# A hybrid decoder layer on one core: modulation weights loaded ahead of x, index scores a unit later with a block in each tile, counts turned later, and the last head's half added ahead of the products

## What is computed

```python
mod = jax.nn.silu(c) @ w_ada + b_ada
shift, scale, gate = jnp.split(mod, 3, axis=-1)
h = rmsnorm(x, norm_in) * (1.0 + scale[:, None, :]) + shift[:, None, :]
(cb, cc, cu, cz, aq, ak, av, az, iq, ik, iw) = jnp.split(h @ w_in, cuts, axis=-1)
y_conv = group_rmsnorm(cb * conv(cc * cu), gn_conv, 8) * jax.nn.silu(cz)
# q, k, q_idx, k_idx are rotated by position (the first 16 of 64 dimensions)
score = sum over 8 index heads of w_idx * relu(q_idx . k_idx)       # causal
_, sel = lax.top_k(score, 256)                 # for every query, in blocks of 128
y_attn = softmax attention of 8 heads over the chosen keys
y_attn = group_rmsnorm(y_attn, gn_attn, 8) * jax.nn.silu(az)
return rmsnorm(x + gate[:, None, :] * (concatenate([y_conv, y_attn]) @ w_out), norm_f)
```

## Time and profile before

| | us |
|---|---|
| median of 3 runs | 781.19 (779.42 to 783.22) |
| the profiled execution | 780.36 |
| its span, first to last instruction | 778.6 |
| PE busy | 674.9 (87%) |
| DVE / ACT / POOL busy | 471.5 / 360.5 / 230.1 |

### The profile page before, as it was taken

The page is one execution under the profiler, slowest core; times in us unless marked ns, Lnnn a source line. Parts: engine busy times, 40 slices in busy tenths (PEclk is TensorE's granted clock), DMA queues, the critical chain, the costliest instruction groups (busy, mean ns, idle before and its releaser), DMA issues.

```text
span 778.6 us, 8765 instructions
## 1 busy us (share of the span) xinstructions
PE 674.9 (87%) x3170; PEld 550.7 (71%) x3170; DVE 471.5 (61%) x734; ACT 360.5 (46%) x542; POOL 230.1 (30%) x111
## 2 busy tenths in 40 slices
PE   0459993989999999639999999999889989879995
PEld 0447993768888888537887877787777777658884
DVE  3677822778889999955802210003788989566734
ACT  3554432755643223413244443344787877773211
POOL 0032322035324225531765656460011310030000
PEclk9967996999999999969999999999999999989998
DMA  8901189024325211100113411124964440211431
GB/s 341 367 28 54 48 218 154 1 81 136 103 88 165 80 55 54 33 22 28 54 63 128 162 55 32 50 64 104 297 154 113 111 106 4 57 55 68 174 109 54
DMA packets 22517, 79.14 MB, mean 102 GB/s; under 512 B 3722, under 2 KB 4042, under 8 KB 21452
## 3 DMA queue, kind: packets, MB, share of 16 engines
q1 hardware_dynamic: 22476, 78.60, 33.3%
HBM read 61.77 MB, written 13.41 MB: 97 GB/s over the span
## 4 chain that ended last, share of the span: by engine, by line
PE 55%; DVE 28%; DMA 5%; issue 5%; ACT 4%; SPq 2%; DVEq 0%; POOL 0%; ACTq 0%
PE ps L615 10%; PE ps L616 10%; PE ps L617 10%; DVE above L1232 7%; PE ps L790 4%; PE ps L792 4%; PE ps L791 4%; PE ps L728 3%; DMA xin<-in_x 2%; PE ps L673 2%; PE ps L674 2%; PE ps L654 2%; DMA iqs<-hlL 2%; PE ps L655 2%; DVE acc L1130 2%
## 5 line engine op out<-in xcount | busy, mean ns | idle before, releaser
L615 PE MATMUL ps<-hH,wH 128*128 128x512 f32 (+1 forms) x592 | 234.2, 396 | 8.4 <-DVE hL L430 4.4
L616 PE MATMUL ps<-hL,wH 128*128 128x512 f32 (+1 forms) x592 | 229.6, 388 | 0.0
L617 PE MATMUL ps<-hH,wL 128*128 128x512 f32 (+1 forms) x592 | 229.5, 388 | 0.0
L1451 POOL TENSOR_TENSOR wL<-raw,wH 128x1024 fp32r<-128x1024 f32 x37 | 93.7, 2534 | 219.1 <-ACT wH L852 219.0
L615 PEld LDWEIGHTS ps<-hH,wH 128*128 128x128 f32 x592 | 112.6, 190 | 33.9 <-issue 11.7
L617 PEld LDWEIGHTS ps<-hH,wL 128*128 128x128 f32 x592 | 112.7, 190 | 21.7
L616 PEld LDWEIGHTS ps<-hL,wH 128*128 128x128 f32 x592 | 113.1, 191 | 19.8 <-issue 1.0
L1317 DVE CUSTOM_DVE_ANT_0 ps<-ps,bias 128x128 f32<-128x128 f32 (+3 forms) x64 | 48.7, 761 | 57.1 <-PE ps L655 55.2
L1325 DVE TENSOR_TENSOR phL<-ps,phH 128x512 fp32r<-128x512 f32 (+1 forms) x96 | 52.7, 555 | 23.9 <-ACT phH L1007 19.1
L987 ACT ACTIVATE relu<-ps,wabs 128x384 f32<-128x384 f32 (+5 forms) x48 | 40.0, 849 | 46.8 <-PE ps L674 27.1
L1232 DVE TENSOR_SCALAR_CACHE_REDUCE above<-score,srch 128x384 bf16<-128x384 f32 (+5 forms) x60 | 56.8, 946 | 2.1
(11 more groups left out here) (193 smaller groups left out, 1073.5 us busy)
## 6 DMA issues: line engine op xcount, KB each, us to landing
raw<-in_w_units SPq DMA_DIRECT2D x36, 512.0 KB, 3.4
wa<-in_w_ada SPq DMA_DIRECT2D x8, 1024.0 KB, 13.3
ks<-qk_halves SPq DMA_DIRECT2D x32, 256.0 KB, 5.5
xin<-in_x SPq DMA_DIRECT2D x8, 512.0 KB, 12.5
gw<-in_w_ada SPq DMA_DIRECT2D x8, 512.0 KB, 4.9
qs<-qk_halves SPq DMA_DIRECT2D x16, 256.0 KB, 3.9
wo<-in_w_out SPq DMA_DIRECT2D x8, 512.0 KB, 9.2
xe<-in_x SPq DMA_DIRECT2D x8, 512.0 KB, 4.1
```

Source lines behind the costliest of these rows:

```text
L615: pe.matmul(out, wH[:, n % 2, kt, :], hH[:, kt, cols], start=(kt == 0), stop=False)
L616: pe.matmul(out, wH[:, n % 2, kt, :], hL[:, kt, cols], start=False, stop=False)
L617: mm = pe.matmul(out, wL[:, n % 2, kt, :], hH[:, kt, cols], start=False, stop=(kt == KT - 1))
L1451: g.tensor_tensor(wL[:, n % 2, :, :], raw[:, n % NRAW, :, :], wH[:, n % 2, :, :].bitcast(F32), ALU.subtract).then_inc(s_wL, 1)
```

## The change

The front: w_ada is loaded whole before x, and x is squared, rooted and normalized in groups of 4, 2, 1 and 1 tiles. PE adds up the modulation first and turns x afterwards; no copy of the turned x is made. ACT makes five tiles of h straight out of PSUM with scale and shift, DVE the tiles 1, 4 and 6 (`H_DVE`), ACT makes all hH, DVE all hL and POOL none. Before unit 0 PE does all 64 transposes, in three PSUM pairs, each of which must have been read before it is used again.

The scores: one block in each of aq1, aq2, aq3, ak1, ak2, ak3; the rotation of ak0 stands before block 2 and no longer behind block 3; the turned rows of iq0 are read back at iq3 instead of aq0. The counts: "most" behind cz1 and cc2, the gate's loads at cz2, cc3, cu3, cb3, its turning behind cz3, its row's way out at az1. The end: `head_out(15)` stands ahead of the scalings, block 3's first part is split into high and low within the last head, early steps are spread otherwise, and block 7 is finished in two halves.

```diff
-        ("aq", 0): [("idx", 2), ("idx", 3)],
-        ("ak", 0): [("idx", 4)],
...
+        ("ak", 0): [("idx", 2)],
+        ("aq", 1): [("idx", 3)],
...
-        ("cb", 0): [("most", 0)],
-        ("cz", 0): [("most", 1)],
-        ("cb", 3): [("gate", 0)],
+        ("cz", 1): [("most", 0)],
+        ("cc", 2): [("most", 1)],
+        ("cz", 3): [("gate", 0)],
...
+SCORES_IN = {UNIT[u]: (i, 1, 4 if i == 2 else 0)
+             for i, u in enumerate((("aq", 1), ("aq", 2), ("aq", 3), ("ak", 1), ("ak", 2), ("ak", 3)), 2)}
+GATE_IN = {UNIT[u]: kt for kt, u in zip(range(0, KT, 2), (("cz", 2), ("cc", 3), ("cu", 3), ("cb", 3)))}
+H_DVE = (1, 4, 6)
+X_GROUPS = ((0, 4), (4, 6), (6, 7), (7, 8))
...
-EARLY_PARTS = {3: 2, 4: 2, 5: 2, 6: 2, 7: 2, 8: 2, 10: 2, 11: 2}
+EARLY_PARTS = {4: 2, 5: 2, 6: 2, 7: 3, 8: 3, 10: 2, 11: 2}
...
-                if UNITS[n] == ("aq", 0):
+                if UNITS[n] == ("iq", 3):
                     sp.wait_ge(s_spill[0], spilled(0))
...
+            for t in range(NB):
+                pe.wait_ge(s_xn, t + 1)
+                for kt in range(3):
+                    mm = turn_x(kt, t)
+                    if t == NB - 1:
+                        mm.then_inc(s_xtp, 1)
+            for kt in range(3, KT):
+                wait_h(pe, kt - 3)
+                for t in range(NB):
+                    mm = turn_x(kt, t)
+                mm.then_inc(s_xtp, 1)
...
+            for kt in range(KT):
+                if kt not in H_DVE:
+                    act.wait_ge(s_xtp, kt + 1)
+                    A(xT[:, kt, :], two(2 + 2 * (kt % 3)), ACT.Identity, bias=shift[:, kt:kt + 1],
+                      scale=amp[:, kt:kt + 1]).then_inc(s_hA, 1)
+                wait_h(act, kt)
+                A(hH[:, kt, :], xT[:, kt, :], ACT.Copy).then_inc(s_hH, 1)
             split_high(1)
...
+            make_h(H_DVE[0])
+            for kt in range(KT):
+                if kt + 2 in H_DVE:
+                    make_h(kt + 2)
+                dve.wait_ge(s_hH, kt + 1)
+                v.tensor_tensor(hL[:, kt, :], xT[:, kt, :], hH[:, kt, :].bitcast(F32), ALU.subtract).then_inc(s_hL, 1)
...
             rotate(TURN_AT[("aq", 0)])
+            rotate(TURN_AT[("ak", 0)])
...
-                if i == 3:
-                    rotate(TURN_AT[("ak", 0)])
...
+            b = NB - 1
+            dve.wait_ge(s_xe[1], 16 * (b // 2 + 1))
+            dve.wait_ge(s_fsq, b)
+            for half in range(2):
+                cols = slice(HALF * half, HALF * half + HALF)
+                if half:
+                    dve.wait_ge(s_op, NB)
+                else:
+                    dve.wait_ge(s_oph, 1)
+                v.tensor_tensor(te[:, 1, cols], ps[:, out_pair(b) + half, :], gate[:, cols], ALU.mult).then_inc(s_teh, 1)
```

More of the change, by code:

```diff
@@ L232, in build @@
         finr = small[:, 48:56]
+        finh = small[:, 56:58]
+        squares = at("squares", [P, 4, D], F32, 32)
         xin = at("xin", [P, NB, D], F32, 113)
@@ L424, in wait_low, with wait_h @@
                 waits.wait_ge(s_splP, m + 1 - NT)
-        def low_h(engine, waits, kt, done):
-            waits.wait_ge(s_h, kt + 1)
-            waits.wait_ge(s_hH, kt + 1)
-            engine.tensor_tensor(hL[:, kt, :], xT[:, kt, :], hH[:, kt, :].bitcast(F32), ALU.subtract).then_inc(done, 1)
+        def wait_h(waits, kt):
+            if kt in H_DVE:
+                waits.wait_ge(s_hD, H_DVE.index(kt) + 1)
+            else:
+                waits.wait_ge(s_hA, kt + 1 - sum(x < kt for x in H_DVE))
         block = ctx.enter_context(nc.Block())
@@ L450, in _ @@
             for kt in range(KT):
-                if kt == 3:
-                    for t in range(NB):
-                        sp.dma_start(xin[:, t, :], a["x"][0, P * t:P * t + P, :]).then_inc(s_x[t], 16)
                 if kt >= 4:
@@ L563, in _ @@
             sp.dma_start(gate[:], dgate.rearrange("(o n) -> o n", o=1).broadcast_to([P, D])).then_inc(s_gate, 16)
-            for b in range(NB):
+            for b in range(NB - 1):
                 sp.wait_ge(s_fin, b + 1)
@@ L569, in _ @@
                     sp.dma_start(xe[:, b % 2, :], a["x"][0, P * (b + 2):P * (b + 3), :]).then_inc(s_xe[b % 2], 16)
-            for i in range(2):
-                sp.wait_ge(s_out[i], 16 * (NB // 2))
+            for half in range(2):
+                sp.wait_ge(s_finh[half], 1)
+                cols = slice(HALF * half, HALF * half + HALF)
+                sp.dma_start(a["out"][0, P * (NB - 1):P * NB, cols], oe[:, 1, cols]).then_inc(s_out[1], 16)
+            sp.wait_ge(s_out[0], 16 * (NB // 2))
+            sp.wait_ge(s_out[1], 16 * (NB // 2 + 1))
         @block.tensor
@@ L593, in _, with turn_x @@
             mm.then_inc(s_modp, 1)
+            def turn_x(kt, t):
+                return pe.transpose(two(2 + 2 * (kt % 3))[:, P * t:P * t + P], xin[:, t, P * kt:P * kt + P], identF[:])
+            for t in range(NB):
[6 more added lines that the diff above has]
+                wait_h(pe, kt - 3)
+                for t in range(NB):
+                    mm = turn_x(kt, t)
+                mm.then_inc(s_xtp, 1)
             def unit(n):
@@ L610, in unit @@
                             pe.wait_ge(s_hH, kt + 1)
-                            if kt in HL_POOL:
-                                pe.wait_ge(s_hLp, HL_POOL.index(kt) + 1)
-                            else:
-                                pe.wait_ge(s_hL, kt + 1 - sum(k < kt for k in HL_POOL))
+                            pe.wait_ge(s_hL, kt + 1)
                         pe.matmul(out, wH[:, n % 2, kt, :], hH[:, kt, cols], start=(kt == 0), stop=False)
@@ L1081, in _ @@
                     high(2, 0)
+                    high(3, 0)
                 if k == LAST // 2 + 10:
@@ L1087, in _ @@
             pair_root(NT - 1, 0)
-            high(3, 0)
             for ct in LATE_OUT:
@@ L1094, in _, with last_block @@
             pair_root(NT - 1, 1)
+            def last_block():
+                for half in range(2):
+                    act.wait_ge(s_resh, half + 1)
+                    cols = slice(HALF * half, HALF * half + HALF)
+                    A(xe[:, 1, cols], te[:, 1, cols], ACT.Square, accum_out=finh[:, half:half + 1]).then_inc(s_fsq, 1)
+                act.wait_ge(s_fv, NB)
+                A(finr[:, NB - 1:NB], fin[:, NB - 1:NB], ACT.Sqrt, scale=1.0 / D, bias=vec[:, V_EPS:V_EPS + 1]).then_inc(s_fs, 1)
+                act.wait_ge(s_fr, 1)
+                act.wait_ge(s_rnh, 2)
+                A(oe[:, 1, HALF:D], oe[:, 1, HALF:D], ACT.Copy, scale=finr[:, NB - 1:NB]).then_inc(s_finh[1], 1)
             for b in range(NB):
```

131 lines of the change are left out of this document (70 added, 61 removed).

## The result

| | before | after |
|---|---|---|
| median of the runs, us | 780.64 (779.42 to 783.22) | 736.28 (735.85 to 738.53) |
| profiled execution, its span | 778.6 | 734.0 |
| mean granted clock | 0.96 | 0.99 |

The ratio is 0.9424, its 95% interval [0.9395, 0.9453]: 5.8% faster. The forecast was 731.0 with a range of 722 to 742, so the sign and the range hold. The sum of the gains was 50.3 us and the spans differ by 44.6. Four cuts through the two traces say where the missing 5.7 went. They are the start of unit 1, PE's first transpose of a block of attention weights (`prob`), the start of the last matmuls of the output, and the end.

A forecast was written before the change was run, and what follows sets the result against it. PE, busy 87% of the span, was taken as the bound, standing still in four places. Gains of 7.8, 12.9, 2.3, 19.4, 5.0, 1.0 and 1.9 sum to 50.3 us: span 778.6 to 728.3, median 731 us, range 722 to 742.

The forecast's parts named there:

- The counts: PE's 17.6 us wait behind cb0 for DVE's count vanishes, plus 1.8 of clock: gain 19.4 us, bounds 14 to 19.4.
- The rival of a longer search: DVE's search stretches beside POOL's work until the count is late again and bounds PE: 737 us, chance 0.10.
- The slices: PE's 12.0 us wait in ak0 for slices of iq nearly vanishes, with its clock loss: gain 12.9 us, bounds 8 to 13.8.
- The start: Before unit 0, ACT's chain of h ends sooner, last hL at 57.5 us against 65.7: gain 7.8, bounds 5 to 10.
- The scores: PE's 3.8 us of relu waits shrink to some 1.5 at block 2: gain 2.3 us, bounds 0 to 3.8.
- The tail: At the attention's end, the squares' wait goes, some 2.2 us for DVE's sum remain: gain 5.0 us, bounds 3 to 7.
- The early steps: Early output steps no longer stand where PE waits 1.8 us for ACT: gain 1.0 us, bounds 0 to 2.5.
- The last block: Block 7's closing full-width steps are done in halves, ending sooner: gain 1.9 us, bounds 1.2 to 2.5.
- The queue: The iq slices are bound by the DMA queue and land only 3 us earlier: 736 to 738 us, chance 0.10.
- The start gains nothing: ACT's chain runs 0.6 us a step slower than added up, hL ends at 65: 738 to 739 us, chance 0.10.
- Slower by SP's wait: SP's wait for the masks at cz2 delays cb3's weights, about 791 us if masks come at 475; chance 0.02.

The follow-up runs named there:

- e2: Changed kernel with scores and the read-back of iq0's rows put back where they stood before, counts left as changed: 748.45 us.
- e1: Changed kernel with only the new start kept, everything else as before the change: 768.46 us, ratio 0.9858 to the kernel before.
- e8: Changed kernel with block 2's scores from step 8 of aq1 instead of 4, and POOL's low part of aq0 held until six scores are done: 742.43 us.
- e10: e7 plus block 2's scores from step 8 of aq1 instead of 4, and aq0's low part made by DVE instead of POOL: 725.86 us.
- e6: Changed kernel with DVE's gate of the last half pair ahead of the four scalings and its sum ahead of w_out's low part: 730.73 us.
- e7: e6 plus POOL's two last low parts of w_out given to DVE, so POOL has no work in the tail: 729.47 us.
- e4: Changed kernel with the end of the attention and the early steps put back as before the change: 734.82 us.
- e3: Changed kernel with the turned counts and the gate's sums put back where they stood before: 772.12 us, ratio 0.9882 to the kernel before.
- e5: Changed kernel with block 7 of the output finished whole instead of in two halves: 737.83 us.

## Why the prediction was right, and where it was not

The total came within 5.3 us, but in part because errors cancel: the start, the slices and the last block gave some 3 us more than forecast, the scores, the counts and the end of the attention with the early steps some 9 us less.

**The counts, right.** Forecast 19.4, measured alone 18.3 to 18.7, with its mechanism: PE is at the count at 358.8, as computed, and the masks are done at 405.2 (forecast 403). The slack was 12.5 us instead of 17, because the count was there at 346.3, not at 341.4: the search started 3.1 us later than computed, and DVE's last row for the count took 2.25 us where it had 0.17 before. The rival of a longer search came only to that extent: 113.7 us from the search's first row to the count's, against 114.0.

**The slices, right, but by the luck of less than 1 us.** No wait for them is left, so the term stands at its upper bound of 13.8, or near it: e2, which takes back slices and scores together, loses 12.2. The forecast kept 1.1 us of the wait "by the old landing". The landing moved some 11.9 us (134.3 to 122.4) instead of the 7.8 plus 0.2 that I gave it: the start gained more (below), and the queue the rest, with a spread of some 0.6 us between executions. The credit for the read-back at iq3 was right to be small: no effect beyond that spread can be seen.

**The start, right, undersized.** 9.9 for 7.8. The last hL was computed for 57.5 and came at 56.05. The step that was off is the roots: I had ACT's squares follow the landings, x7's root near 40.2, but it ended at 38.98, since a square and its read-out took some 1.15 one behind the other, less than the 1.28 that I set. The chain of h took 13.9 us, as forecast, by two errors that cancel: the passes that read PSUM with scale and bias from a tile took 1.19 to 1.21 and not 1.03, and the high parts in a row 1.00 and not 1.06. Of the missing 2.1 us, this is 1.45. Another 0.4 was lost in writing the forecast down: its own 65.7 less 57.5 is 8.2, not 7.8. The last 0.2 is unit 0, 6.4 us from the last hL to unit 1 in place of 6.6; PE's clock is 1.00 from 30 us on (0.52 from 45 to 62 us before), but before it waited for hL anyway and had caught up as well. And e1 shows the part alone at 12.2, 2.4 of it by a search that ran shorter.

**The scores, wrong in size: 2.3 forecast, nothing gained.** The step that failed is "PE stops for some 1.5 us". It stopped for 3.07 and then ran at a granted clock of 0.83 over ten us in the profiled execution. I had put the rotation's last addition in at 3.29 but its neighbours at their own times; DVE's first score behind it, 0.41 by itself, took 2.49 beside POOL's low part. e8 and e10 show that: take POOL's instruction away and the row is 0.41. The trace of before had the same pair right behind the row, and the forecast did not use it:

```profile
159.62 2.65 DVE L1206 TENSOR_SCALAR score<-relu,wsgn 128x640 f32<-128x640 f32 x1
158.58 3.35 POOL L417 TENSOR_TENSOR hlL<-T,hlH 128x1024 fp32r<-128x1024 f32 x1
```

**The tail, wrong in size: 5.0 forecast, next to nothing gained.** The four scalings and the sum were right. The step that failed is "the gate (0.7), a low part of w_out (1.25 [...], longer while POOL works)". The words had the cause and the number left it out: they took 2.90 and 3.37, 4.3 us more than the 1.95 summed. The trace of before had both instructions, in this same tail and beside work of POOL:

```profile
693.95 2.06 DVE L1377 TENSOR_TENSOR hL<-wo,woB 128x1024 fp32r<-128x1024 f32 x1
695.93 2.85 DVE L1355 SCALAR_TENSOR_TENSOR ya<-ya,vec,azs 128x512 f32<-128x512 f32 x1
```

With these two prices, 4.91 us for the 1.95, the sum lands 3.0 us later and the wait for it is 5.2 instead of 2.2, more than the 4.0 of the squares that it replaces; it measured 4.86. (The forecast's terms add up to 695.3 where it wrote "near 696"; from 695.3 the wait would be 4.4.) That the cause is POOL is shown (e6: 0.75 for the same gate; e7: four low parts at 1.2). The rule cited with the search, that a DVE instruction with two SBUF inputs and a GpSimd one that reads SBUF exclude each other for the whole instruction (the Trainium skill, SBUF — State Buffer, Who interferes with whom), holds for the gate and the low part, and belonged in this term. The first score is no exception to it: the same section counts `tensor_scalar` among the operations that can take the shared ports with one SBUF input, and the 2.49 us beside POOL against 0.41 alone agree.

**The early steps** were not measured apart; with the tail they brought 0.8 of 6.0, and e4, which takes both back, is as fast.

**The last block, right.** 2.2 for 1.9.

**The rivals.** "The queue" came within 0.3 to 0.7 us of deciding. "The start gains nothing" is disproved by e1. "Slower by SP's wait" needed masks 62 us late; they were 2 us late. That the parts do not add up was nowhere in the forecast, and did no harm only because all parts were in: with the counts left out the change would have given 8.5 us (e3), less than the start gives by itself.

**Open.** How much of the scores' loss is the wait and how much the clock is not settled, since the clock behind the same wait differs: I can't say why e4's execution had the clock at 1.00 from 130 to 140 us, with the same instructions and the same wait of 3.1 us before it as the changed kernel's at 0.83 (e5, e6 and e7, with that wait too, have 0.83):

```profile
130.00:140.00 10.00, 7.93 (x36) 6.77 (x37) 6.68 (x10) 6.23 (x9) 2.06 (x3) 1.00 0.39 132
130.00:140.00 10.00, 8.09 (x30) 6.95 (x31) 6.28 (x10) 4.83 (x8) 0.97 (x1) 0.83 0.37 121
```

The first row is e4's, the second the changed kernel's. It is worth 1.4 us: everything behind is that much earlier, the first turned `prob` at 502.3 for 503.7. So a wait of this length sometimes costs the clock and sometimes not, and a forecast can only have it in its range.

## What to carry to other kernels

When steps are reordered so that a small DVE instruction is the one PE waits for, price every DVE row ahead of it with what POOL does at that time, at the price of a row of the trace that stood beside POOL, not at its own. The best such row is the same instruction in the kernel before, read where it stands now; if the two engines share such a stretch, DVE alone can be quicker than both. Before giving a part of a change a gain, ask which wait it stands in front of: the same move was worth 18 us or 36, and moving scores later gained nothing until nobody waited for the search. Holding work back to clear another engine's way pays only if no buffer hangs on that work (e8).
